# Gathering expert tokens as quarter rows for 32x32 transposes on VectorE, with the down products one expert behind

## The reference

```python
scores = sigmoid(t @ w_router)                 # 64 experts in 8 groups
top_e = top 6 experts out of the 4 best groups # per token
gates = scores[top_e] / sum * 2.5
for e in range(64):                            # tokens grouped by expert
    y = (silu(t[tok_e] @ we_gate[e]) * (t[tok_e] @ we_up[e])) @ we_down[e]
    acc[tok_e] += y * gate
out = layer_norm(2 ** 0.25 * t + shared_mlp(t) + acc)
```

## Time and profile before

| | us |
|---|---|
| median of 3 runs | 3145.42 (3142.37 to 3145.54) |
| span of the profiled execution, first to last instruction | 3143.6 |
| experts in the profile: up products of the first to down products of the last | 1824 to 3066 |

### The profile page before, as it was taken

One profiled execution on the slowest core, in us unless ns is written; L12 is line 12 of the kernel. 1 busy time (PEld: TensorE's weight loads), 2 busy tenths in 40 slices (PEclk: granted clock), 3 DMA queues, 4 the chain that ended last, 5 costly groups with the idle time before them and its releaser, 6 DMA issues.

```text
span 3143.6 us, 38160 instructions
## 1 busy us (share of the span) xinstructions
PE 3083.4 (98%) x14334; PEld 1978.5 (63%) x14334; DVE 1105.1 (35%) x3389; ACT 689.7 (22%) x1569; POOL 641.6 (20%) x632
## 2 busy tenths in 40 slices
PE   8999999999999999999999999999999999999998
PEld 4445555554445555554556777877787777878775
DVE  6422433330026767763777421111111111111115
ACT  2311111110015455541111011111111111111114
POOL 3300000000000110101454212222222223223325
PEclk9999999999999999999999999999999999999999
DMA  6421010001000103006444577887887888888886
GB/s 226 153 70 28 14 28 14 1 14 54 20 7 6 50 11 109 11 8 212 145 138 149 180 224 228 233 241 237 242 246 238 241 241 265 265 267 269 270 245 238
DMA packets 179112, 458.82 MB, mean 146 GB/s; under 512 B 24944, under 2 KB 97472, under 8 KB 153192
## 3 DMA queue, kind: packets, MB, share of 16 engines
q1 hardware_dynamic: 133872, 339.23, 30.5%
q0 software_dynamic: 42752, 108.72, 15.7%
q10 hardware_dynamic: 2304, 8.39, 0.7%
HBM read 342.33 MB, written 113.92 MB: 145 GB/s over the span
## 4 chain that ended last, share of the span: by engine, by line
PE 53%; DVE 0%; POOL 0%; issue 0%; ACT 0%
PE ps L2403 23%; PE ps L2335 11%; PE ps L2190 7%; PE ps L2319 4%; PE ps L2246 3%; PE ps L2332 2%; PE ps L2256 1%; PE ps L2209 1%; PE ps L2279 0%; PE ps L2200 0%; POOL moe_fin L1983 0%; PE ps L2177 0%; PE ps L2230 0%; PE ps L2219 0%; DVE moe_fin L1647 0%
## 5 line engine op out<-in xcount | busy, mean ns | idle before, releaser
L697 PE MATMUL ps<-ret_w,hT 128*128 128x512 f32 (+1 forms) x1088 | 465.0, 580 | 0.0
L2403 PEld LDWEIGHTS ps<-moe_xT,moe_wg 128*128 128x128 f32 x2048 | 352.7, 196 | 44.8 <-issue 40.8
L2403 PE MATMUL ps<-moe_xT,moe_wg 128*128 128x192 f32 (+22 forms) x2048 | 378.4, 338 | 0.0
L2403 PE MATMUL ps<-moe_xT,moe_wu 128*128 128x192 f32 (+22 forms) x2048 | 375.2, 336 | 0.0
L2335 PE MATMUL ps<-moe_wd,moe_hh 128*128 128x512 f32 (+12 forms) x800 | 366.5, 601 | 1.0 <-DVE moe_hh L1456 0.8
L2403 PEld LDWEIGHTS ps<-moe_xT,moe_wu 128*128 128x128 f32 x2048 | 353.3, 196 | 4.3
L1924 POOL DMA_INDIRECT base_rows<-moe_yo,index x100 | 164.7, 1647 | 847.3 <-DVE moe_yo L1565 717.2
L697 PEld LDWEIGHTS ps<-ret_w,hT 128*128 128x128 f32 (+1 forms) x1088 | 195.5, 185 | 223.0 <-issue 215.9
L1456 DVE TENSOR_TENSOR moe_hh<-moe_sl,ps 128x256 f32<-128x256 f32 (+19 forms) x144 | 53.7, 373 | 769.7 <-ACT moe_sl L2042 747.8
L2335 PEld LDWEIGHTS ps<-moe_wd,moe_hh 128*128 128x128 f32 (+12 forms) x800 | 136.6, 181 | 159.3 <-issue 149.8
L1057 PE MATMUL ps<-hT,fox_w 128*128 128x512 f32 (+1 forms) x576 | 229.2, 560 | 0.0
(11 more groups left out here) (255 smaller groups left out, 3572.5 us busy)
## 6 DMA issues: line engine op xcount, KB each, us to landing
moe_wg<-in_we_gate SPq DMA_DIRECT2D x64, 1024.0 KB, 5.0
moe_wu<-in_we_up SPq DMA_DIRECT2D x64, 1024.0 KB, 7.0
moe_wd<-in_we_down SPq DMA_DIRECT2D x64, 1024.0 KB
fox_c<-ck SPq DMA_DIRECT2D x8, 1032.0 KB, 8.4
emb_xin<-in_x SPq DMA_DIRECT2D x16, 512.0 KB, 3.9
h_rows<-emb_hr SPq DMA_DIRECT2D x16, 512.0 KB, 2.8
ret_w<-in_w_in SPq DMA_DIRECT2D x16, 512.0 KB, 6.5
moe_yt<-h_rows SPq DMA_DIRECT2D x16, 512.0 KB, 5.0
```

The costliest lines, as they stand in the source:

```text
L697: ins = pe.matmul(ps[0:n, g % 2, lo:hi], hT[:, c, t0:t0 + n], wr[u][:, c, lo:hi], start=(c == 0), stop=(c == DC - 1))
L2403: ins = pe.matmul(out, w[:, c, f:FF:FC], xT[u][:, c, 0:n], start=(c == 0), stop=(c == DC - 1))
```

## The change

- **Gathers.** `t_rows` is read as `quarters`, 8192 rows of 1 KB. An indirect DMA now takes 32 tokens: partition group q (32 partitions) gets quarter q of each. `index4` holds 4 x token + q for it. Expert i needs `SUBS[i]` = ceil(c/32) gathers, 9 down to 6, 433 in all (13856 slots). `xg` becomes 24 buffers of 256 values a partition, in the room of 6 of 1024. They stay on POOL, now three experts ahead.
- **Transposes.** `turn_rows(i)` on DVE writes each of them to `xT` with one instruction of 32x32 transposes, 128x256 elements. `turn` on PE and both `x_copy` are gone, and with them banks 0 and 1 as a way station. It waits for the up products of expert i-2 and all gathers of i, and stands ahead of `product(i-1)`.
- **Index.** PE's `turn_lists` first does 9 more small products, from `lists4`, a copy of the lists repeated four times by ACT (`copy_lists`); DVE makes `index4` of them. `lists4` lies in the room of the second down weights.
- **Order.** PE does the up products of expert i, then the down products of i-1; DVE and ACT evict i-1 after the product of i. SP loads up weights of i, then down weights of i-1.

```diff
--- before
+++ after
...
 SLOTS = SEQ + P
+QP = 32
+NQ = P // QP
+QD = D // NQ
+SUBS = [-(-c // QP) for c in CAPS]
+NSUB = SUBS[0]
+WIDE = [sum(s > j for s in SUBS) for j in range(NSUB)]
+AT4 = [sum(WIDE[:j]) for j in range(NSUB + 1)]
 SPARE = NK * P
...
         yd_upto = [sum(not x for x in packed[:g]) for g in range(NBLK + 1)]
-        NXG, NYO, NYT = 6, 4, 4
-        CMAX = CAPS[0]
+        NXG, NYO, NYT, NRI = 24, 4, 4, 4
+        CMAX = QP * NSUB
+        s0 = [sum(SUBS[:i]) for i in range(NE + 1)]
 
...
             wu[u] = sb(f"wu{u}", [P, DC, FF], over=early)
+            l4 = [early[0]]
             wd[u] = sb(f"wd{u}", [P, FC, D], over=early)
+        lists4 = sb("lists4", [NE, P * NSUB], over=l4)
         over = [start]
...
         at[0] = rows_at[0]
-        xg = [sb(f"xg{r}", [P, D]) for r in range(NXG)]
+        xg = [sb(f"xg{r}", [P, QD]) for r in range(NXG)]
         tail = [start]
...
         halves = base_rows.rearrange("r (h d) -> (r h) d", h=2)
+        quarters = t_rows.rearrange("r (q d) -> (r q) d", q=NQ)
         rows = lambda ap, i: ap[i * P:(i + 1) * P, :]
...
                 gates, gates2 = ps[:, 7, 0:NK * NE], ps[:, 7, NK * NE:(NK + E2) * NE]
+                dve.wait_ge(quartered, 1)
+                dve.tensor_scalar(route.index4[:, :], ps[:, 1, 0:AT4[NSUB]], float(NQ), route.quarter,
+                                  ALU.mult, ALU.add).then_inc(indexed4, 1)
                 dve.wait_ge(turned_l, 1)
...
 
-            def x_copy(g):
-                i, k, m = BLK[g]
-                dve.wait_ge(turned, 2 * g + 2)
-                dve.tensor_copy(xT[i % 2][:, 4:8, k * P:k * P + m],
-                                ps[:, 1, :].rearrange("p (c t) -> p c t", c=4)[:, :, 0:m]).then_inc(xT_d, 1)
+            def turn_rows(i):
+                dve.wait_ge(gu, FC * (SH + i - 1))
+                dve.wait_ge(rows_in[i % NRI], 16 * sum(SUBS[i % NRI:i + 1:NRI]))
+                for x in range(SUBS[i]):
+                    r = (s0[i] + x) % NXG
+                    dve.transpose(xT[i % 2][:, :, QP * x:QP * (x + 1)],
+                                  xg[r][:, :].rearrange("p (t c) -> p c t", c=DC)).then_inc(xT_d, 1)
 
...
             shared_evict(3)
-            last = HB + 2 * (SH - 1)
-            x_copy(0)
-            shared_part(last, 0)
-            x_copy(1)
-            shared_part(last, 1)
-            x_copy(2)
-            shared_part(last + 1, 0)
-            shared_part(last + 1, 1)
+            turn_rows(0)
+            shared_evict(SH - 1)
             n_over = overflow_count(dve)
-            for i in range(NE):
-                c = CAPS[i]
-                product(SH + i, c, lambda f: ps[:, 2 + f, 256:256 + c] if c <= 256 else ps[:, 4 + f, 0:c])
-                nxt = list(range(b0[i + 1], b0[i + 2])) if i + 1 < NE else []
-                own = list(range(b0[i], b0[i + 1]))
-                for x in range(max(len(nxt), len(own))):
-                    if x < len(nxt):
-                        x_copy(nxt[x])
-                    if x < len(own):
-                        evict(own[x])
+            for i in range(NE + 1):
+                if i + 1 < NE:
+                    turn_rows(i + 1)
+                if i < NE:
+                    c = CAPS[i]
+                    product(SH + i, c, lambda f: ps[:, 2 + f, 256:256 + c] if c <= 256 else ps[:, 4 + f, 0:c])
+                for g in (range(b0[i - 1], b0[i]) if i >= 1 else []):
+                    evict(g)
 
...
 
-            def weights(i):
-                u = i % 2
-                e = sp.value_load(route.order[0:1, i:i + 1], min_val=0, max_val=NE - 1)
-                one = lambda w, c: w[bass.ds(e, 1)].rearrange("a (p c) f -> p (a c) f", c=c)
+            def expert(i):
+                return sp.value_load(route.order[0:1, i:i + 1], min_val=0, max_val=NE - 1)
+
+            def one(w, e, c):
+                return w[bass.ds(e, 1)].rearrange("a (p c) f -> p (a c) f", c=c)
+
+            def up_weights(i):
+                u, e = i % 2, expert(i)
                 if i >= 2:
                     sp.wait_ge(gu, FC * (SH + i - 1))
-                sp.dma_start(wg[u][:, :, :], one(we_gate, DC)).then_inc(wgu_in[u], 16)
-                sp.dma_start(wu[u][:, :, :], one(we_up, DC)).then_inc(wgu_in[u], 16)
+                sp.dma_start(wg[u][:, :, :], one(we_gate, e, DC)).then_inc(wgu_in[u], 16)
+                sp.dma_start(wu[u][:, :, :], one(we_up, e, DC)).then_inc(wgu_in[u], 16)
+
+            def down_weights(i):
+                u, e = i % 2, expert(i)
                 if i >= 2:
                     sp.wait_ge(down, b0[i - 1])
-                sp.dma_start(wd[u][:, :, :], one(we_down, FC)).then_inc(wd_in[u], 16)
+                sp.dma_start(wd[u][:, :, :], one(we_down, e, FC)).then_inc(wd_in[u], 16)
 
...
             sp.wait_ge(ordered, 1)
-            weights(0)
+            up_weights(0)
             shared_t(4)
-            weights(1)
+            up_weights(1)
+            down_weights(0)
+            sp.wait_ge(quartered, 1)
+            down_weights(1)
             n_over = overflow_count(sp)
-            for i in range(2, NE):
-                weights(i)
+            up_weights(2)
+            for i in range(3, NE):
+                up_weights(i)
+                down_weights(i - 1)
+            down_weights(NE - 1)
             sp.dma_start(grow2[:, :], ln2_g.partition_broadcast(P)).then_inc(const2, 16)
...
             def gather(i):
-                for g in range(b0[i], b0[i + 1]):
-                    _, k, n = BLK[g]
-                    r = g % NXG
+                for x in range(SUBS[i]):
+                    g = s0[i] + x
                     if g >= NXG:
-                        pool.wait_ge(turned, 2 * (g - NXG) + 2)
-                    pool.indirect_dma_start(out=xg[r][0:n, :], out_offset=None, in_=t_rows,
+                        pool.wait_ge(xT_d, g - NXG + 1)
+                    pool.indirect_dma_start(out=xg[g % NXG][:, :], out_offset=None, in_=quarters,
                                             in_offset=bass.IndirectOffsetOnAxis(
-                                                ap=route.index[0:n, k * NE + i:k * NE + i + 1], axis=0)
-                                            ).then_inc(rows_in[r], 16)
+                                                ap=route.index4[:, AT4[x] + i:AT4[x] + i + 1], axis=0)
+                                            ).then_inc(rows_in[i % NRI], 16)
 
...
                 scatter(i)
-            pool.wait_ge(indexed, 2)
+            pool.wait_ge(indexed4, 1)
             for r in range(NYT):
                 pool.wait_ge(t_out[r], 16 * (NX // NYT))
             gather(0)
             gather(1)
+            pool.wait_ge(indexed, 2)
             n_over = overflow_count(pool)
             for r in range(NYO):
                 pool.wait_ge(base_out[r], 16 * (NX // NYO))
+            gather(2)
             for i in range(NE):
-                if i + 2 < NE:
-                    gather(i + 2)
+                if i + 3 < NE:
+                    gather(i + 3)
                 add_rows(i)
...
 
-            def x_copy(g):
-                i, k, n = BLK[g]
-                act.wait_ge(turned, 2 * g + 1)
-                nc.scalar.copy(xT[i % 2][:, 0:4, k * P:k * P + n],
-                               ps[:, 0, :].rearrange("p (c t) -> p c t", c=4)[:, :, 0:n]).then_inc(xT_a, 1)
+            def copy_lists():
+                act.wait_ge(listed, 16)
+                nc.scalar.copy(lists4[:, :].rearrange("e (j q t) -> e j q t", q=NQ, t=QP),
+                               lists[:, 0:QP * NSUB, 0].rearrange("e (j t) -> e j t", t=QP).unsqueeze(2).to_broadcast([NE, NSUB, NQ, QP])
+                               ).then_inc(copied_l, 1)
 
...
             sigmoid(NX - 1)
-            for s in range(2, SH):
-                silu(s, SW)
-                base_store(s - 1)
-            for g in range(b0[1]):
-                x_copy(g)
+            silu(2, SW)
+            base_store(1)
+            silu(3, SW)
+            copy_lists()
+            base_store(2)
+            silu(4, SW)
+            base_store(3)
             base_store(SH - 1)
             act.wait_ge(weighted, 2)
             n_over = overflow_count(act)
-            for i in range(NE):
-                silu(SH + i, CAPS[i])
-                nxt = list(range(b0[i + 1], b0[i + 2])) if i + 1 < NE else []
-                own = list(range(b0[i], b0[i + 1]))
-                for x in range(max(len(nxt), len(own))):
-                    if x < len(nxt):
-                        x_copy(nxt[x])
-                    if x < len(own):
-                        evict(own[x])
+            for i in range(NE + 1):
+                if i < NE:
+                    silu(SH + i, CAPS[i])
+                for g in (range(b0[i - 1], b0[i]) if i >= 1 else []):
+                    evict(g)
 
...
                 pe.wait_ge(slotted, NX)
+                pe.wait_ge(copied_l, 1)
+                for j in range(NSUB):
```

(67 more changed lines are left out.)

## The result

The kernel after takes **3021.7 us** (median of 4 runs, 3019.1 to 3023.6) against 3145.5 of the kernel before beside it: ratio 0.9611 [0.9598, 0.9625], 124 us faster. The forecast was 3046, with a range from 3026.

A forecast was written before the change was run, and what follows sets the result against it. TensorE was taken to set the pace, with the DMA engines a near second limit. Turns -118.5, edges +2.3, +1.2, +1 and +2, DMA +13 sum to -99 us from 3145.4: forecast 3046, range 3026 to 3115.

The forecast's parts named there:

- part 4: DMA engines: 1 KB gather packets at 60 ns each put the last 28 experts at the edge, 13 us lost.
- the reorder taken at 0: On TensorE, down products of expert i-1 after the up products of expert i were costed at 0.
- Part 1: TensorE loses its transposes of gathered rows in 129 blocks, all on its path: 118.5 us gained; reorder costed at 0.
- a change of kind that stays: On TensorE, the first down block's 3.66 us against the second's 3.44 was expected to remain after the reorder.
- Part 2: VectorE's 433 transposes, taken at 0.40 us each (ends 0.33 and 1.1), stay hidden: cost 0.
- Part 3: POOL's gathers and adds, 13.1 us against a new loop of 18.5, stay hidden; gathers stand three experts ahead.
- the need "as measured": DMA engine time per expert from measured busy shares, 17.6 us at capacity 212; this upper figure loses 23 us in all.
- The lower figure of 2 us: DMA engines kept fed: the last eight experts lose 0.2 to 0.4 us each, 2 us in all.
- B: On the DMA engines a 1 KB packet costs about 110 ns: 60 us lost, so 3095; chance 0.22.
- C: On the DMA engines a 1 KB packet costs 160 ns: 113 us slower plus the edges, 3265; chance 0.13.
- Part 5: Edges of the expert stretch: list products +2.3, VectorE's transposes +1.2, late gathers +1, tail +2 us.

The follow-up runs named there:

- r7: Kernel before with the new order of up and down products and gathers three experts ahead, turns still on TensorE: 3132.8 us, ratio 0.9974.
- r2: Kernel after with the old order, each expert's down products right after its own up products: 3085.0 us, ratio 0.9818.
- r3: Kernel after with the earlier gathers of 4 KB rows and one VectorE transpose a block, 129 for 433: 3016.9 us, ratio 0.9604.
- r12: Kernel after with gathers two experts ahead instead of three: 3319.8 us, ratio 1.0574 to the kernel before.
- r4: Kernel after with gathered pieces of 768 bytes instead of 1 KB, a quarter of each row left out: 3034.1 us, ratio 0.9654.
- r5: Kernel after with two more 256 KB loads in each expert, into a tile nothing reads: 3036.1 us, ratio 0.9663.
- r6: Kernel after with expert 0's transposes spread between the last four shared evictions and down products of 62 ahead of up products of 63: 3019.8 us.
- r1: Kernel before with the new order alone, turns still on TensorE, gathers two experts ahead: 3268.5 us, ratio 1.0402.
- r8: Kernel after with expert 0's transposes spread, layer-norm constants and tail's shared rows loaded earlier: 3030.4 us; again on another chip 3015.9.

## Why the prediction was right, and where it wasn't

The lower end of the range, 3026, is the turns' gain with every loss at nothing (3145.4 less 118.5 is 3026.9). So the measured 3021.7 can't come from a smaller loss alone: with the 13 us of part 4 at 0 the sum gives 3033. Two steps failed, the reorder taken at 0 and the DMA term.

- **Part 1, the turns.** Right: r7, which has order and lead but keeps the turns, takes 1229.2 us from first up to last down product, the kernel after 1112.3. That is 116.9 us for its 126 turns, where the forecast's prices make 115.8 (118.5 less 2.7 for the three ahead of the first expert).
- **Part 1, the reorder "at 0"; "a change of kind that stays".** This step failed: the 3.66 against 3.44 went with the old order (r7), 12.2 us over the experts (1241.4 less 1229.2; 0.22 x 62 would be 13.6). The forecast had priced activation and product at 0.4 each and held that the turn covers both; r2 shows 1.1 for both with the gaps around them, more than the turn's 0.89. Reckoned so, the wait could have been seen: 3.66 stood only where a wait was possible.
- **Part 2.** Right in effect: the transposes are hidden (r3). One takes 603 ns (median of 433) where 0.40 was taken, within its ends. The Trainium skill (VectorE: DVE Perf Modes, "The three transpose paths") has 311 ns for 128 columns of bf16; for twice the columns, in f32, this trace shows 1.9 times that. The advice of the same page ("Rules for kernel authors") to leave such transposes on TensorE would have cost 117 us here (r7 against the kernel after).
- **Part 3.** Right: a gather takes 0.95 us and 0.30 between, all hidden. But the part named the lead of three experts without a price. It carries the change: by the ratios, r12 is some 300 us behind the kernel after.
- **Part 4, "I take 13 us".** Failed: 0. Both of its props fell. The pieces don't travel alone: the sizes in the trace show four in a packet of 4096 bytes (r4), and the queue's packets take no more time in all than before, so 60 ns a packet times 4 was no price; and the need "as measured", share times time, is not a limit, since TensorE never waits at a share of 1.03 and still has room at 346 GB/s (r5). The lower figure of 2 us was the better one. For rivals B and C this removes the ground too: they needed 110 and 160 ns for packets of 1 KB, which don't exist.
- **Part 5.** Small and too small: the front +3.3 where +1.8 follows from its terms (4.5, less 2.7 for three turns there). The new list products took 2.0 us where 2.3 was forecast; the other 1.5 of the lists are clock, which no term had and which is chance as far as these runs show (r6 has 0.3 of it). VectorE's stall was 2.7, not 1.2, at 0.53 us a transpose and with evictions queued behind. For late gathers, priced at 1 us, the trace shows no wait. The tail was +3.8, not +2.

Together: 12.2 us of order, 1.1 of turns and 13 of DMA, less 3.3 at the edges (1.5 and 1.8), are 23 of the 25 us; the rest is within what runs differ by. The losses at the edges hid a part of what the two failed steps gave.

## What to carry to other kernels

When a step is pushed one iteration back, go through every queue that waits for it, and ask how long the loads queued behind have left: here a lead of two or three experts decides between -4% and +6%. A wait of TensorE's can cost more than its length: in r1 and r12 the slower products at the lower clock added about a half (43 to 90 us) and over a third (80 to 215) of the waits. Where the same instruction costs a few tenths more in one place than in another, ask which wait could end just there, before calling it a change of kind. A DMA share near 1 isn't proof of a full DMA engine; TensorE's waits are what tells, and a dummy load beside it measures the room.

## What the runs showed that was not expected

- The pieces of a gather share packets, four of 1 KB in each, or six and two of 768 bytes. Gathers of 1 KB pieces land sooner than those of whole rows did: median 5.0 us from issue, 8.5 before.
- The DMA share of a window can be over 1 (1.03 at 323 GB/s).
- TensorE can stand still for its own issue for 1 to 2 us at a time, with nothing in the profile that it waits for (r8: 8.2 us in 55); the same kernel on another chip has none of it. The cause is open.
- The same list products take 6.41 us in the kernel after and 5.15 in r6, at granted clocks of 0.71 and 0.95, with TensorE busy throughout in both.
